# The norms of block two: GpSimd multiplies the branch by its root and splits the second unit's weights

## The reference, cut to what matters

```python
for layer in range(DEPTH):
    h = rmsnorm(x, norm_mix_pre[layer])
    m = mixer(h)                       # starts with h @ w_in
    x = x + rmsnorm(m, norm_mix_post[layer])
    h = rmsnorm(x, norm_ffn_pre[layer])
    f = (silu(h @ w_gate) * (h @ w_up)) @ w_down
    x = x + rmsnorm(f, norm_ffn_post[layer])
```

## Time and profile before

| | |
|---|---|
| median of 3 runs (lowest to highest) | 2487.73 us (2485.97 to 2489.97) |
| the profiled execution's own time | 2485.94 us |
| its span, first to last instruction | 2484.1 us |
| TensorE busy | 2314.3 us (93%) |
| VectorE busy | 1321.7 us (53%) |
| ScalarE busy | 961.7 us (39%) |
| GpSimd busy | 181.3 us (7%) |
| mean granted TensorE clock | 0.985 |
| chain that ended last | PE 75%, DVE 9%, ACT 5% |

### The profile page before, as it was taken

How to read it: one execution, slowest core, us unless ns; L and a number is a source line. 1 busy time by engine, 2 the same in 40 slices (tenths; PEclk the granted TensorE clock), 3 DMA queues, 4 the chain that set the end, 5 groups by cost and what they waited for, 6 DMA issues and landing times.

```text
span 2484.1 us, 41855 instructions
## 1 busy us (share of the span) xinstructions
PE 2314.3 (93%) x16984; PEld 1816.9 (73%) x16984; DVE 1321.7 (53%) x2005; ACT 961.7 (39%) x1603; POOL 181.3 (7%) x229
## 2 busy tenths in 40 slices
PE   6999999887989999877999989999999989999999
PEld 4777777676857766666766657888887657888887
DVE  4336643676275653666467755555425764555522
ACT  3225444353343444344445544222223554222222
POOL 0000000363000000263000000000000010000000
PEclk9999999998999999999999999999999999999999
DMA  7721111000212111100322212333333222333332
GB/s 265 266 78 42 35 37 54 27 4 20 60 35 74 40 47 47 43 4 12 110 60 60 60 43 68 93 101 93 98 95 106 58 66 70 94 101 93 97 94 80
DMA packets 300524, 182.01 MB, mean 73 GB/s; under 512 B 5290, under 2 KB 284476, under 8 KB 300236
## 3 DMA queue, kind: packets, MB, share of 16 engines
q1 hardware_dynamic: 286940, 150.50, 20.9%
q10 hardware_dynamic: 12480, 25.17, 2.8%
q0 software_dynamic: 944, 4.07, 0.5%
HBM read 177.60 MB, written 2.12 MB: 72 GB/s over the span
## 4 chain that ended last, share of the span: by engine, by line
PE 75%; DVE 9%; ACT 5%; issue 4%; DVEq 3%; POOL 2%; POOLq 1%; ACTq 1%; DMA 0%; SPq 0%
PE PW L325 12%; PE PW L327 12%; PE PW L326 12%; PE PW L415 6%; PE PW L416 5%; PE PW L417 5%; PE PW L1269 2%; PE PW L1226 2%; PE PW L1817 1%; DVE wlo L247 1%; PE PW L3008 1%; PE PW L600 1%; PE PW L982 1%; POOL BK L2051 1%; PE PW L570 1%
## 5 line engine op out<-in xcount | busy, mean ns | idle before, releaser
L247 DVE TENSOR_TENSOR wlo<-wraw,whi 128x1024 fp32r<-128x1024 f32 (+1 forms) x272 | 329.5, 1212 | 379.1 <-ACT whi L240 356.1
L240 ACT ACTIVATE whi<-wraw 128x1024 fp32r<-128x1024 f32 (+1 forms) x272 | 283.7, 1043 | 266.8 <-PE PW L327 256.4
L415 PE MATMUL PW<-hhi,whi 128*128 128x512 f32 (+1 forms) x880 | 324.3, 369 | 11.7 <-DVEq L3217 7.0
L325 PE MATMUL PW<-hhi,whi 128*128 128x512 f32 (+1 forms) x824 | 315.0, 382 | 0.0
L326 PE MATMUL PW<-hhi,wlo 128*128 128x512 f32 (+1 forms) x824 | 314.7, 382 | 0.0
L327 PE MATMUL PW<-hlo,whi 128*128 128x512 f32 (+1 forms) x824 | 314.6, 382 | 0.0
L416 PE MATMUL PW<-hhi,wlo 128*128 128x512 f32 (+1 forms) x880 | 306.5, 348 | 0.0
L417 PE MATMUL PW<-hlo,whi 128*128 128x512 f32 (+1 forms) x880 | 306.4, 348 | 0.0
L415 PEld LDWEIGHTS PW<-hhi,whi 128*128 128x128 f32 x880 | 167.9, 191 | 57.2 <-issue 24.0
L416 PEld LDWEIGHTS PW<-hhi,wlo 128*128 128x128 f32 x880 | 168.3, 191 | 21.9 <-issue 3.3
L417 PEld LDWEIGHTS PW<-hlo,whi 128*128 128x128 f32 x880 | 167.9, 191 | 22.0
(11 more groups left out here) (478 smaller groups left out, 4134.9 us busy)
## 6 DMA issues: line engine op xcount, KB each, us to landing
wraw<-in_w_in SPq DMA_DIRECT2D x68, 512.0 KB, 3.9
mod_w<-in_mod_w ACTq DMA_DIRECT2D x12, 2048.0 KB, 10.6
wraw<-in_ffn_w_gate SPq DMA_DIRECT2D x44, 512.0 KB, 3.8
wraw<-in_ffn_w_up SPq DMA_DIRECT2D x44, 512.0 KB, 3.8
wraw<-in_ffn_w_down SPq DMA_DIRECT2D x32, 512.0 KB, 4.0
wraw<-in_attn_w_in SPq DMA_DIRECT2D x24, 512.0 KB, 3.9
wraw<-in_w_out SPq DMA_DIRECT2D x16, 512.0 KB, 4.0
wraw<-in_rg_w_in SPq DMA_DIRECT2D x16, 512.0 KB, 3.9
```

The source lines that it names most:

```text
L240: act.activation(whi[:, slot, 0:kb, :], wraw[:, slot, 0:kb, :], ACT.Copy).then_inc(S("w_hi"), 1)
L247: dve.tensor_tensor(wlo[:, slot, 0:kb, :], wraw[:, slot, 0:kb, :], whi[:, slot, 0:kb, :].bitcast(F32), ALU.subtract).then_inc(S("w_split"), 1)
L325: pe.matmul(acc, wh[:, k, :], rhi[:, k0 + k, s0:s1], start=a, stop=False)
L415: e.matmul(acc, whi[:, u % 2, k, :], rhi[:, k0 + k, s0:s1], start=k == 0, stop=False)
```

## The change

In each of the four ramps GpSimd gets a program (`Ramp.pool`). It waits for the branch's root, does the `lo_part` of the second unit's weights that DVE did, and then makes the products of branch and root for blocks 2 to 7. DVE still makes the products of blocks 0 and 1; for the others it waits for GpSimd's signal `ramp_branch`, and goes straight to the multiply-add. There are two product buffers: GpSimd writes that of block b when x of block b-2 is done. The matmuls of the squares stay where they were. In the attention phase GpSimd's ramp stands ahead of its mask, in the recurrence's phase behind its two DMAs.

```diff
@@ class Ramp, __init__
-                (self.summed1, self.rooted1, self.xnew, self.squared, self.summed,
-                 self.rounded, self.low, self.rooted) = (Signal(n_, c) for n_, c in (
+                (self.summed1, self.rooted1, self.xnew, self.squared, self.summed, self.rounded, self.low, self.rooted,
+                 self.branch) = (Signal(n_, c) for n_, c in (
...
+                     ("ramp_branch", NB - 2)))
+            def pool(self, g, st):
+
+                def multiplied(b):
+                    g.wait_ge(self.xnew.sem, self.xnew.at(b - 1))
+                    g.tensor_tensor(self.halves(self.tmp[:, b % 2, :]), self.halves(self.m[:, b, 0:SEQ]), self.root1, ALU.mult) \
+                     .then_inc(self.branch.sem, 1)
+                g.wait_ge(self.rooted1.sem, self.rooted1.at(1))
+                lo_part(g, 0, st, 1, st["body"][1])
+                for b in range(2, NB):
+                    multiplied(b)
@@ class Ramp, dve
                 for b in range(NB):
-                    if b == 1:
-                        lo_part(v, 0, st, 1, st["body"][1])
-                    v.tensor_tensor(self.halves(self.tmp[:, b % 2, :]), self.halves(self.m[:, b, 0:SEQ]), self.root1, ALU.mult)
-                    v.drain()
+                    if b < 2:
+                        v.tensor_tensor(self.halves(self.tmp[:, b, :]), self.halves(self.m[:, b, 0:SEQ]), self.root1, ALU.mult)
+                        v.drain()
+                    else:
+                        v.wait_ge(self.branch.sem, self.branch.at(b - 1))
@@ attn2
             def pool_program(pool):
+                ramp.pool(pool, st)
                 pool.wait_ge(S("bias_tile"), 16)
@@ ffn
-            gate_and_up = dict(sp=lambda sp: sp_stage(sp, st_gu), pe=pe_program, act=act_program, dve=dve_program)
+            gate_and_up = dict(sp=lambda sp: sp_stage(sp, st_gu), pool=lambda g: ramp.pool(g, st_gu), pe=pe_program, act=act_program, dve=dve_program)
```

More of the change, by code:

```diff
@@ L964, in __init__ @@
                 self.tmp = arena(f"branch_{name}", [P, 2, SEQ], off=65 * K1)
-                (self.summed1, self.rooted1, self.xnew, self.squared, self.summed,
-                 self.rounded, self.low, self.rooted) = (Signal(n_, c) for n_, c in (
+                (self.summed1, self.rooted1, self.xnew, self.squared, self.summed, self.rounded, self.low, self.rooted,
+                 self.branch) = (Signal(n_, c) for n_, c in (
                      ("post_summed", 1), ("post_rooted", 1), ("post_x", NB), ("pre_squares", NB),
-                     ("pre_summed", NB), ("pre_rounded", NB), ("pre_low", NB), ("pre_rooted", 1)))
+                     ("pre_summed", NB), ("pre_rounded", NB), ("pre_low", NB), ("pre_rooted", 1),
+                     ("ramp_branch", NB - 2)))
             def ready(self, k):
```

## The result

The changed kernel takes 2505.43 us (median of 6 runs, 2501.94 to 2507.84), the kernel before 2487.91 us (6 runs, 2483.02 to 2489.97). The ratio is 1.0072, with a 95% interval of 1.0059 to 1.0085. The forecast was 2498.2, with 2487 to 2507 as its range: the direction and the mechanism came out, the size was 10.3 us forecast against 17.5 measured (14.7 to 21.1 by the interval of the ratio).

A forecast was written before the change was run, and what follows sets the result against it. TensorE was taken to bound the kernel, delayed by DVE in four ramps. DVE and GpSimd taking turns, DVE first, with the clock's fall, cost 4 x 2.63 = 10.5 us: 2498.2 on the median's scale, range 2487 to 2507.

The forecast's parts named there:

- What bounds the ramp: Four ramps: DVE's chain leads to the first matmul; then DVE's cycle of 2.27 us and TensorE's 2.24 are nearly equal.
- Exclusion: In the ramps: DVE instructions with two SBUF inputs and GpSimd's tensor_tensor take turns, holding about 0.55 to 0.6 and 1.15 us.
- The start: Ahead of the first matmul: GpSimd's split holds up DVE's product of block 1; TensorE starts at 1231.6 or 1232.55, against 1229.89.
- the order that it gave second: Ramp's start: GpSimd's product of block 3 goes ahead of DVE's low part of block 0; TensorE starts at 1232.55.
- The signs: Ramp's trace if right: L1009 and L1022 means well above 0.75 us, GpSimd's split 2.3 to 2.4, first matmul 6.8 to 8.
- Who goes first: Low part of block 0 against GpSimd's product of block 3: DVE was taken first, with TensorE starting at 1231.6, not 1232.55.
- one of its rivals: In the ramps: GpSimd goes first and the clock falls, 4 x 3.6 us more, 2502.1; chance 0.18 for 2502.1 and above.
- The cycle: Per block of the ramp: GpSimd's product 1.15, two DVE instructions of 0.6, drain 0.1, together 2.45 us against 2.27.
- The clock: Each ramp: TensorE's pause grows from 1.52 to 3.2 to 4.2 us, clock halves for 3.4 us, TensorE loses 1.67.
- a rival of double length: In the ramps: a clock fall of double length costs another 6.7 us, 2504.9 or 2508.8; within 0.18 for 2502.1 and above.
- Nothing behind the ramp takes it up: Behind each ramp: order is as before and TensorE leads, so a ramp's delay passes on to the end in full.

The follow-up runs named there:

- early_split: Kernel before, GpSimd idle, with the second unit's rounding (ACT) and split (DVE) moved ahead of the wait for the branch's root: 2477.66 us, ratio 0.9979.
- longer_spin: Changed kernel with 40 useless matmuls in place of 24 behind the branch's last sum of squares in each ramp: 2499.14 us, ratio 1.0060 to the kernel before.
- idle_tensor_tensor: Kernel before plus six GpSimd tensor_tensor products of 128x512 per ramp, root by root, whose result nobody uses: 2501.59 us, ratio 1.0070.
- idle_tensor_scalar: Kernel before plus unused GpSimd tensor_scalar instructions (root times a gain column) in each ramp, six of 128x512: 2489.81 us, ratio 1.0013.
- early_and_products: Kernel before with the second unit's rounding and split ahead of the root on ACT and DVE, and products of blocks 2 to 7 on GpSimd: 2492.22 us, ratio 1.0024.

## Why the prediction was right, and where its size was off

- **What bounds the ramp**: right for the start, where DVE's chain leads up to the first matmul (early_split took 1.12 us off it and the ramp became 1.13 shorter). Behind the first matmul it is right for the first ramp alone. In the other three the chain of the kernel before runs through TensorE from the first matmul on; here it is in the second ramp (start us, us, what):

```profile
1524.57 0.76 DVE hlo L1022
...
1525.46 0.47 PE PW L287
...
1527.09 0.86 PE PW L982 x2
...
1529.33 0.86 PE PW L982 x2
```

The prediction worked the first ramp out and multiplied by four. The first one takes 23.80 us before (the 23.96 has its end from the chain, 0.16 later than the timeline's), the others 23.4, so what DVE's longer cycle costs is 0.4 us more in each of those: 3.54 and then 3.9 in longer_spin.
- **Exclusion**: right, and shown twice, by the changed kernel and by idle_tensor_tensor, where no data passes between the engines inside the ramp. The rule of the Trainium skill ("SBUF — State Buffer", "Who interferes with whom") holds for scalar_tensor_tensor against tensor_tensor: 1.57 us for 0.75. For GpSimd's tensor_scalar it overstates what happened here, 0.94 for 0.75.
- **The start**: right to 0.1 us for the order that it gave second. Forecast with GpSimd first 1232.55 - 1224.60 = 7.95, measured 8.02. The steps agree too, so this is no luck: from the first product to the end of GpSimd's split 3.85 forecast and 3.76 measured, to the end of DVE's product of block 1 4.4 and 4.31.
- **The signs**: two of them came out otherwise. GpSimd's split was to take 2.3 to 2.4 us and took 2.77, since it began beside a DVE instruction. And the multiply-adds were to have a mean well above 0.75; it is 0.85, one of 1.58 and seven of 0.74 per ramp. Only one DVE instruction per cycle meets a GpSimd product, the low part (mean 1.42), because the product is released by the multiply-add.
- **Who goes first**: wrong. "I take DVE first" rested on a drain of 0.1 us against a release that the prediction left unsized: GpSimd's product starts 0.08 us behind the multiply-add's end, 0.01 to 0.02 ahead of the low part, in every block that both want. By the prediction's own sum this is 0.95 us per ramp (no kernel with DVE first was run), and with it the forecast would have been 2502.1, one of its rivals.
- **The cycle**: 2.58 in place of 2.45. The term that was too small is the product: 1.15 us, read from products that had been waiting, where a product that finds the way free takes 1.27 to 1.29 from its start. The rest of the cycle, 0.08 for the release, 0.55 and 0.66 for DVE's two instructions, is 1.29 against 1.3. The trace of before had the longer product: the shortest of the gate's six (L3053) takes 1.28.
- **The clock**: the fall was right, its length and its price weren't. The prediction took 3.4 us in each ramp; it was 3.4 in the first and 6.8 in the other three, which the text held as a rival of double length (2504.9 and 2508.8). With GpSimd first it priced a fall at 0.8 us and a double one at 1.67 more; against longer_spin the fall cost 0.35 us in the first ramp and 1.39, 1.21 and 1.57 in the others. That it costs less than was priced fits two things: TensorE is idle in a part of the double falls (5.55 us busy of 6.70 in the second ramp), and its own 2.24 us per block leave it waiting in a cycle of 2.58. Neither was tested alone.
- **Nothing behind the ramp takes it up**: right. The stretches between the ramps differ by at most 0.3 us from those of before.

So the mechanism held and the size did not: per ramp 2.6 us were forecast, and 3.9, 5.3, 5.1 and 5.5 measured. The steps that failed are the choice of order, the length of the product and the length of the fall. The first and the third had been worked out and taken as the less likely. The measured 2505.43 lies near the upper end of the range, 2507, and the interval of the measurement (14.7 to 21.1 us) reaches past that end: that it fell inside is in part luck.

## What to carry to other kernels

An idle GpSimd is not a second DVE: its tensor_tensor and a DVE instruction with two SBUF inputs take turns, so in these ramps moving such work between them took no time off the path, and each piece is about twice as long there (0.69 to 1.28, 1.23 to 2.35 by the row of block one). Before work is moved to another engine, see whether its own engine stands idle ahead of the same wait: there the split cost nothing. And where two engines are released by one signal and then exclude each other, price both orders, and take the cheaper one only if a row shows it.

## What the runs showed that was not expected

TensorE's pause ahead of the ramp against the granted clock in it, over all nine kernels: with pauses of 0.25, 0.67, 1.52 and 1.69 us the clock stayed up in every ramp; with 2.15, 2.36, 3.18 and 3.64 it was at the lower level for 3.4 us in every ramp (one of the four pauses of idle_tensor_tensor was 2.34 in place of 3.18); with 4.24 for 3.4 in one and for 6.8 in three. Why the same pause gave two lengths stays open. One kernel alone, longer_spin, changes the pause and nothing else. A window over most of a ramp for one pause and inside the low stretch for the other, idle_tensor_scalar (1.69) and early_and_products (2.15):

```profile
1529.00:1548.00 19.00, 19.00 (x64) 1.00 0.05 12
```

```profile
1524.40:1527.70 3.30, 3.30 (x7) 0.50 0.00 0
```

A GpSimd tensor_scalar of 128x512 took 1.57 us in block one and 2.30 us in idle_tensor_scalar. There every DVE instruction beside it has two SBUF inputs; in block one only some have, others read PSUM. Why it slows, and costs DVE only 0.19 us per cycle, stays open.
